# Three unused matmuls ahead of each chunk's norm sum, in the first unit behind each pre-norm

## The reference, cut to what matters

```
h = _rmsnorm(x, norm_mix_pre);  y, states = token_mixers(h);  x += _rmsnorm(y, norm_mix_post)
h = _rmsnorm(x, norm_mlp_pre);  u = square(relu(h @ w_up));   x += _rmsnorm(u @ w_down, norm_mlp_post)

def _rmsnorm(x, g):
    xf = xf * lax.rsqrt(jnp.mean(xf * xf, axis=-1, keepdims=True) + NORM_EPS)
    return (xf * g)
```

## Time and profile before

| what | value |
|---|---|
| median of three runs | 3311.73 us |
| the profiled execution: time / span | 3308.99 us / 3307.3 us |
| TensorE matmul busy | 3127.6 us, 95% |
| VectorE / ScalarE busy | 1987.9 us, 60% / 1423.1 us, 43% |
| mean granted TensorE clock | 0.985 |
| share of TensorE in the chain that ended last | 76% |

### The profile page before, as it was taken

The page is one execution under the profiler, slowest core; times in us unless marked ns, Lnnn a source line. Parts: engine busy times, 40 slices in busy tenths (PEclk is TensorE's granted clock), DMA queues, the critical chain, the costliest instruction groups (busy, mean ns, idle before and its releaser), DMA issues.

```text
span 3307.3 us, 72069 instructions
## 1 busy us (share of the span) xinstructions
PE 3127.6 (95%) x23264; PEld 3062.7 (93%) x23264; DVE 1987.9 (60%) x4003; ACT 1423.1 (43%) x3148; POOL 171.0 (5%) x225
## 2 busy tenths in 40 slices
PE   5999999999999999999969999999989999999997
PEld 5888898998999999999958989999989999999997
DVE  5777765666555545455567777566665455454555
ACT  4555543344433434334345555334444333343333
POOL 0111111110000000000011111111000000000000
PEclk9999999999999999999979999999999999999998
DMA  3334444553454444444424344545435545444444
GB/s 133 126 129 131 132 154 156 167 160 127 156 169 160 167 161 165 165 165 166 153 72 132 124 133 135 162 153 183 152 115 170 167 160 168 161 165 165 165 165 147
DMA packets 266059, 499.23 MB, mean 151 GB/s; under 512 B 34272, under 2 KB 39552, under 8 KB 265664
## 3 DMA queue, kind: packets, MB, share of 16 engines
q1 hardware_dynamic: 243360, 443.56, 40.9%
q0 software_dynamic: 14496, 51.05, 4.6%
q10 hardware_dynamic: 8064, 2.80, 0.3%
HBM read 475.30 MB, written 22.01 MB: 150 GB/s over the span
## 4 chain that ended last, share of the span: by engine, by line
PE 76%; DVE 12%; issue 5%; ACT 3%; DMA 2%; DVEq 1%; ACTq 0%; SPq 0%; POOLq 0%; POOL 0%
PE PU L461 68%; PE PABCD L461 4%; DVE WL L1126 2%; PE PE_ L461 2%; DMA RAW<-in_w 2%; PE PF L461 2%; ACT WH L793 1%; ACT AE L793 1%; DVE Y L1140 1%; DVE Y L1291 1%; DVE PMS L1410 1%; PE PABCD L464 1%; DVE AE L1482 1%; DVE X L1143 0%; DVE Y L1316 0%
## 5 line engine op out<-in xcount | busy, mean ns | idle before, releaser
L461 PE MATMUL PU<-HH,WH 128*128 128x288 f32 x4096 | 1284.8, 314 | 59.1 <-DVE HL L1131 47.8
L793 ACT ACTIVATE WH<-RAW 128x512 fp32r<-128x512 f32 x1669 | 964.6, 621 | 635.5 <-PE PU L461 462.8
L461 PE MATMUL PU<-HL,WH 128*128 128x288 f32 x4096 | 1212.5, 296 | 0.0
L461 PE MATMUL PU<-HH,WL 128*128 128x288 f32 x4096 | 1208.5, 295 | 0.0
L1126 DVE TENSOR_TENSOR WL<-RAW,WH 128x512 fp32r<-128x512 f32 x1668 | 1084.5, 694 | 184.7 <-ACT WH L793 172.3
L461 PEld LDWEIGHTS PU<-HH,WH 128*128 128x128 f32 x4096 | 774.7, 189 | 79.0 <-DVE HL L1131 49.2
L461 PEld LDWEIGHTS PU<-HL,WH 128*128 128x128 f32 x4096 | 776.2, 190 | 7.1
L461 PEld LDWEIGHTS PU<-HH,WL 128*128 128x128 f32 x4096 | 775.0, 189 | 0.0
L461 PE MATMUL PU<-UH,WH 128*128 128x288 f32 x2560 | 759.0, 296 | 3.2 <-DVE UL L1280 2.0
L461 PE MATMUL PU<-UL,WH 128*128 128x288 f32 x2560 | 755.2, 295 | 0.0
L461 PE MATMUL PU<-UH,WL 128*128 128x288 f32 x2560 | 752.7, 294 | 0.0
(11 more groups left out here) (245 smaller groups left out, 2279.9 us busy)
## 6 DMA issues: line engine op xcount, KB each, us to landing
RAW<-in_w SPq DMA_DIRECT2D x1669, 256.0 KB, 3.8
SIN<-in_sin POOLq DMA_DIRECT2D x32, 512.0 KB, 4.3
out_sout<-Y POOLq DMA_DIRECT2D x32, 512.0 KB, 5.4
BC<-gate_rows POOLq DMA_DIRECT2D x32, 304.0 KB, 4.1
AUX<-in_aux POOLq DMA_DIRECT2D x32, 152.0 KB, 3.5
X<-in_x SPq DMA_DIRECT2D x4, 576.0 KB, 7.6
out_y<-X SPq DMA_DIRECT2D x4, 576.0 KB, 2.8
Y<-in_gw POOLq DMA_DIRECT2D x2, 1024.0 KB, 5.1
```

The source lines that it names most:

```text
L461: return nc.tensor.matmul(out, lhsT, rhs, start=start, stop=stop, skip_group_check=True)
L793: return nc.scalar.activation(out, in_, f, **kw)
```

## The change

Ahead of every norm sum in slots 0 to 7 of these quads, TensorE issues three more matmuls: the high weights of chunk 2t (`WH[0]`) against `HH` of that chunk, into `PF`. Each starts its own accumulation and nothing reads the result. The operands were already used by the slot's own unit, and no wait is added.

```
                     for c in (2 * t, 2 * t + 1):
+                        for k in range(3):
+                            mm(PF[:, 0:T], WH[0][:, 2 * t], HH[:, 2 * t])
                         norm_sum(2 * l + (1 if kind == "up_first" else 0), c, c % 4, c == 0, c == NC_ - 1)
```

## The result

The changed kernel takes 3326.81 us (median of 9 runs, 3315.56 to 3334.22), the kernel before in the same comparison 3311.73 us (9 runs, 3309.88 to 3320.48). The ratio is 1.0039, 95% interval 1.0024 to 1.0054: slower by 8 to 18 us, which holds the forecast of 18.0 us only at its edge. The profiled execution of the changed kernel took 3328.39 us, with a span of 3326.7 us.

A forecast was written before the change was run, and what follows sets the result against it. TensorE bounds the kernel, busy 95% of the span, though VectorE sets the pace in "up_first". 12.6 + 2.5 + 2.9 = 18.0 us on 3311.7 gives 3329.8 us; range 3324 to 3335 us, the forecast case's own 3326 to 3333.

The forecast's parts named there:

- The price of a filler: Each added matmul costs TensorE 0.132 us, like a unit matmul, with no cost for switching between float32r and float32.
- the rival that I gave 0.06: Each of 64 new changes of matmul kind costs up to 0.10 us, 6.4 us more, giving 3336 us; chance 0.06.
- the 16.8 us of the prediction: Whole-kernel addition if a filler took the skill's estimated 0.1225 us, instead of 18.0 us at 0.132.
- The first stages: Quad "first" in both layers: 48 fillers each, all on TensorE's path, 6.3 us per stage, 12.6 us together.
- I expect the half-clock stretch to end when it did: In the "first" stages half clock ends at the same time, so the whole addition is paid at full clock.
- up_first: Quad in both layers, from first matmul to `S`: partly hidden in waits, 2.5 us longer in layer 0, 2.9 in layer 1.
- 8 x 2.55 = 20.4 us of work at full clock: In "up_first", eight slots of 2.55 us on TensorE without waits, against 19.6 us before.
- The loss at half clock: In "up_first", TensorE loses 1.7 us in layer 0 and 2.1 in layer 1, and can no longer catch up.
- The carry: Behind the edited stages, a later `S` or gates' product delays everything after it; TensorE's chain to 1646 us keeps its length.
- the us that I had allowed: Sign of a wrong prediction: the gates' chain behind "first" shortens or lengthens by more than a us.
- The allowance of 2 us for the clock: Over the kernel, 2 us to either side for half-clock stretches that vary at the four places.
- The rival "faster": Later TensorE restarts make half-clock stretches in the heads disappear; 7 us faster with half of 50 us regained, 3305 us; chance 0.02.

The follow-up runs named there:

- The doubling: The changed kernel with six fillers ahead of each norm sum instead of three; 3364.16 us, ratio 1.0129 to the kernel before.
- e2_up_only: The changed kernel with its fillers only in the two quads of kind up_first; 3330.68 us, ratio 1.0023 to the kernel before.
- e11_after_heads: The changed kernel with unused matmuls added ahead of waits in gated-delta, retention and mLSTM heads; 3332.28 us, ratio 1.0043 to the kernel before.

## Why the prediction was right, point by point

- **The price of a filler** was right: 0.132 us from the earlier trace rows, 0.40 us for three in the profile after. The doubling shows the slope, and that switching between kinds costs nothing, the rival that I gave 0.06. The estimate from the Trainium skill, "TensorE: Matmul & The Clock Gate", section Back-to-back issue gap, 0.1225 us, is 7% below what the trace shows. Worked through both kinds of stage that figure gives some 16.3 us, and not the 16.8 us of the prediction.
- **The first stages** were right in kind and 1.5 us off in sum in this pair of profiles (11.1 instead of 12.6). The term that failed is "I expect the half-clock stretch to end when it did". It ended 0.9 us earlier in layer 0 and after 3.95 instead of 5.95 us in layer 1; half of each, 0.45 and 1.0 us, is the difference to 6.3. Taking off half of the time at half clock, by the trace's record of the granted clock, shows that the rest was right. In layer 1 this leaves 28.4 to 28.5 us in five profiles without fillers in the stage and 34.7 to 34.8 us in four with three of them, 6.3 us apart. The half clock itself lasted 3.6 to 6.0 us in the five and 3.1 to 5.9 in the four, so its length varies without the change too, and no effect of the change on it was shown.
- **"up_first"** was right in sum (5.35 us measured, 5.4 forecast). With fillers the stage is 21.04 to 21.13 us plus half of its time at half clock, in eight stages of four profiles (the changed kernel twice, e2_up_only, e11_after_heads). For the 3.57 and 4.37 us that the prediction took, that is its 2.5 and 2.9 us. The make-up was wrong. The step was "8 x 2.55 = 20.4 us of work at full clock" against an elapsed 19.6, which gives 0.8 us without half clock. At full clock it is 1.75 us (22.16 against 20.41), because TensorE does not work without a wait: its first slot lasts 3.73 us, 1.2 us over 2.55, until the second square is there. The loss at half clock, for which I took 1.7 and 2.1 us, was 1.2 and 0.65 on top of that, since the same wait hides the rest. That the two errors cancel is so only where the stage begins at half clock, as it did in both kernels.
- **The carry** was right: a later `S` and a later gates' product move everything behind them, and both MLPs kept their lengths to 0.1 us. The gates' chain, from VectorE's step to the first use of the loaded `BC`, took 39.5 and 40.1 us before and 40.0 and 39.7 us after, within the us that I had allowed.
- **The allowance of 2 us for the clock** failed. It covered the four restarts and left out the short half-clock stretches in the heads. In the nine profiles of kernels without fillers in the heads, the heads of a layer took between 754.7 and 768.6 us. The rival "faster" named these stretches as a gain only, and as something that the change would have to bring about. They vary without the change, in the kernel before by 16 us between two profiles.
- So the time of 3326.81 us, 3 us under the forecast, is in part luck: the stages were 1.5 us short of the forecast in this pair, and the heads' lengths change from one execution to the next by more. Over all profiles the stages come out nearer. The mean first stage of layer 0 is 37.02 us in five profiles with three fillers against 30.97 in seven without; with layer 1's (36.94 against 30.95, in four and five) and the two "up_first" (23.49 and 23.11 against 20.40) that makes 17.8 us for the forecast 18.0, or a ratio of 1.0054. The ratios of the two comparisons, 1.0039 and 1.0061, stand on both sides of it.

## What to carry to other kernels

Cut both spans at marks around each edited place before believing a difference: here one kernel's two profiles differ by as much as the change is worth, while its edited stages repeat to 1.3 us, and to 0.1 us once half of their time at half clock is taken off. When filler work goes into a stage that waits for others, look for the slots in which it no longer waits, here the last two; fillers cost their full price there, whatever the mean slack says. Unused matmuls paid where they stood in waits in which the clock can fall (TensorE's 1 to 3 us waits in the heads, 0.2 to 0.4% here), and cost where TensorE is the bound.

## What was not expected of the hardware

A head with a half-clock stretch is longer by more than the clock alone takes. Two windows from one retention head's scale step to the next, in the kernel before (the changed kernel has the same pair, 37.60 and 34.41 us):

```profile
546.69:583.95 37.26, 34.72 (x248) 33.36 (x247) 21.07 (x36) 13.24 (x28) 4.74 (x6) 0.95 0.49 155
2153.48:2187.51 34.03, 33.31 (x248) 31.88 (x247) 20.62 (x36) 13.45 (x28) 5.03 (x6) 1.00 0.55 171
```

The same 248 matmuls take 1.4 us more of busy time at a mean clock of 0.95, and the head is 3.2 us longer; the other 1.8 us is idle time of TensorE. The wait for ScalarE's spread at slot 8, in the kernel before:

```profile
525.99 0.87 PE L464 MATMUL PABCD<-c_ident,Y 128*128 128x128 f32 x3 [3.07 <-ACT Y L793]
...
2168.07 0.52 PE L464 MATMUL PABCD<-c_ident,Y 128*128 128x128 f32 x3 [0.58 <-ACT Y L793]
```

The long wait stands ahead of the fall of the clock at 526.0 us: TensorE was idle from 522.9 us on. It also comes without a fall, as ahead of 489.85 us (2.54 us, clock 1.00), so the half clock does not make it. What goes with it is VectorE's last addition ahead of the spread, and when GpSimdE's multiplication beside it begins:

```profile
522.85 1.92 POOL L394 TENSOR_TENSOR Y<-SIN,BC 128x1024 f32<-128x1024 f32 x1
523.54 1.86 DVE L1316 TENSOR_TENSOR Y<-AE 128x576 f32<-128x576 f32 x1
...
2166.71 0.76 DVE L1316 TENSOR_TENSOR Y<-AE 128x576 f32<-128x576 f32 x1
...
2167.64 2.21 POOL L394 TENSOR_TENSOR Y<-SIN,BC 128x1024 f32<-128x1024 f32 x1
```

In both profiles of the kernel before and the first of the changed one there are 24 such pairs. In 7 GpSimdE began after the addition had, which then took 0.76 us; in 17 it began ahead of it, and the addition took 1.81 to 2.53 us. All of these heads' waits of over 2 us are among the 17, and none of the 7 is over 0.93 us. No run here moves GpSimdE's work, so this is read from the rows and not tested; nor did I settle why the next heads of the same kind tend to repeat it.

That work in such a wait keeps the clock up was shown: with fillers there the heads had 0 to 2 half-clock stretches a layer beside the long one in the gates' chain, in five layers of ten none, where the 18 layers without had 1 to 7. In the first kernel of them the retention heads' waits were 1.0 to 1.9 us.

The clock also fell after TensorE had been busy for 16 us and then idle for 2.3, within the stage that followed (in two profiles), and did not when twelve more matmuls had cut the gap to 1.5 us (in one). The length of the gap alone does not decide it: in the kernel before TensorE waited 3.59 us ahead of 1742.82 us, and the clock stayed at 1.00. The Trainium skill, "TensorE: Matmul & The Clock Gate", section Why this matters for your kernels, asks for matmul bursts without long idle gaps between them. The trace agrees where the clock fell in or behind waits of 2 to 3 us, and does not where it stayed up behind 3.59 us.
